# Attention with two accumulator banks for two query rows in turn, scores computed three chunks ahead, and the first loads in parts

## What is computed

```python
def mla_block_attend(qn, qp, kn, kp, v, qpos, kpos):
    s = jnp.einsum('bqhd,bkhd->bhqk', qn, kn) + jnp.einsum('bqhr,bkr->bhqk', qp, kp)
    s = jnp.where(chunk_mask(qpos, kpos), s.astype(F32) * MLA_SCALE, NEG_INF)
    p = jax.nn.softmax(s, axis=-1).astype(v.dtype)
    return jnp.einsum('bhqk,bkhd->bqhd', p, v)

def mla_prompt(q_nope, q_pe, ckv, kpe, w_ukv, pos):
    kv = jnp.einsum('bsl,lhe->bshe', ckv, w_ukv)
    k_nope, v = kv[..., :MLA_NOPE], kv[..., MLA_NOPE:]
    ...
    for i in range(q_nope.shape[1] // QBLK):
        lo, hi = i * QBLK, (i + 1) * QBLK
        outs.append(mla_block_attend(q_nope[:, lo:hi], q_pe[:, lo:hi], k_nope[:, :hi], kpe[:, :hi],
                                     v[:, :hi], pos[lo:hi], pos[:hi]))
```

## Time and profile before

| | us |
|---|---|
| median of 3 runs (lowest, highest) | 3652.87 (3643.95, 3655.99) |
| the profiled execution, its time | 3626.36 |
| its span | 3624.6 |
| attention stage: first load issued, first matmul, last output | 1550.3, 1566.0, 2300.8 |
| the steps of the first turn | 1585 to 1748.8 |
| TensorE busy, whole span | 3138.2 (87%) |
| VectorE busy, whole span | 1518.5 (42%) |

### The profile page before, as it was taken

One profiled execution on the slowest core, in us unless ns is written; L12 is line 12 of the kernel. 1 busy time (PEld: TensorE's weight loads), 2 busy tenths in 40 slices (PEclk: granted clock), 3 DMA queues, 4 the chain that ended last, 5 costly groups with the idle time before them and its releaser, 6 DMA issues. The chain is left out here.

```text
span 3624.6 us, 83086 instructions
## 1 busy us (share of the span) xinstructions
PE 3138.2 (87%) x31099; PEld 2434.5 (67%) x31100; DVE 1518.5 (42%) x3411; ACT 1060.9 (29%) x2630; POOL 499.9 (14%) x797
## 2 busy tenths in 40 slices
PE   5999999999999999669898989699809999999980
PEld 5988888888888888535555555355407776777660
DVE  0455555555455544458686868322320000000007
ACT  1333333333333333334434444122202222222220
POOL 0100111011011100100000000011142222222220
PEclk9999999999999999789999999899959999999995
DMA  5100000000000000020101010333218797773336
GB/s 168 28 25 25 25 25 25 28 25 25 25 25 25 27 25 25 22 61 1 35 1 35 1 33 1 120 127 129 102 49 282 230 349 236 250 231 80 82 64 214
DMA packets 136065, 297.66 MB, mean 82 GB/s; under 512 B 29404, under 2 KB 87038, under 8 KB 121342
## 3 DMA queue, kind: packets, MB, share of 16 engines
q1 hardware_dynamic: 113629, 215.78, 17.5%
q0 software_dynamic: 19520, 67.15, 8.0%
q10 hardware_dynamic: 2592, 9.96, 0.7%
HBM read 208.32 MB, written 84.53 MB: 81 GB/s over the span
## 5 line engine op out<-in xcount | busy, mean ns | idle before, releaser
L699 PE MATMUL mx_bank<-mx_xT,mx_w_in 128*128 128x128 f32 (+1 forms) x5440 | 677.3, 282 | 25.7 <-DMA mx_w_in<-in_w_in 25.2
L699 PEld LDWEIGHTS mx_bank<-mx_xT,mx_w_in 128*128 128x128 f32 (+1 forms) x5440 | 633.3, 191 | 92.9 <-issue 84.2
L1397 PE MATMUL at_bank<-at_kT,at_qT 128*128 128x512 f32 (+5 forms) x656 | 295.6, 537 | 2.4 <-DVE at_vals L1521 2.4
L1369 ACT ACTIVATE at_PQ<-at_bank,at_nms 128x512 f32<-128x512 f32 (+5 forms) x328 | 193.0, 596 | 280.4 <-DVE at_nms L1497 199.6
L2185 DVE SCALAR_TENSOR_TENSOR ex_th<-ex_th,ex_bank 128x256 f32<-128x256 f32 x64 | 26.9, 421 | 581.6 <-ACT ex_th L2101 581.6
L2172 PE MATMUL ex_bank<-ex_wd,ex_hT 128*128 x512 | 234.1, 600 | 2.1 <-ACT ex_hT L2107 2.1
L2152 PE MATMUL ex_bank<-ex_wg,ex_xT 128*128 x1024 | 234.6, 383 | 1.2 <-SPq L2022 1.2
L2152 PEld LDWEIGHTS ex_bank<-ex_wg,ex_xT 128*128 128x128 f32 x1024 | 196.6, 192 | 55.4 <-issue 31.3
L2152 PE MATMUL ex_bank<-ex_wu,ex_xT 128*128 x1024 | 231.5, 379 | 0.0
L1428 PEld LDWEIGHTS at_bank<-at_PT,at_vals 128*64 128x64 f32 (+1 forms) x2208 | 118.5, 138 | 160.5 <-issue 82.4
L1540 DVE COPY at_PT<-at_bank 128x512 f32<-128x512 f32 (+3 forms) x328 | 196.7, 601 | 57.1 <-PE at_bank L1409 43.1
(11 more groups left out here) (308 smaller groups left out, 5041.4 us busy)
## 6 DMA issues: line engine op xcount, KB each, us to landing
ex_wg<-in_w_eg SPq DMA_DIRECT2D x32, 1024.0 KB
ex_wu<-in_w_eu SPq DMA_DIRECT2D x32, 1024.0 KB
ex_wd<-in_w_ed SPq DMA_DIRECT2D x32, 1024.0 KB
mx_x<-in_x SPq DMA_DIRECT2D x19, 512.0 KB, 4.6
ro_x<-in_x SPq DMA_DIRECT2D x17, 512.0 KB, 3.7
scr_hx<-ro_h SPq DMA_DIRECT2D x17, 512.0 KB, 2.7
scr_acc<-ro_ha SPq DMA_DIRECT2D x17, 512.0 KB, 3.0
co_r<-scr_acc SPq DMA_DIRECT2D x17, 512.0 KB, 3.7
```

Of the source, the lines that this page charges most:

```text
L699: ins = pe.matmul(dst, w_in[:, k, col:col + n], xT[:, k, :], start=(k == 0), stop=(k == KC - 1))
L1369: ins = a.activation(PQ[:, n % NP, 0:full], b[:, 0:full], ACT.Exp, bias=bias, scale=SCALE, accum_out=sums[:, j, h, 1 + gi:2 + gi])
L1397: t.mark(pe.matmul(bank[n % SB][:, 0:wd], qT[h][keys(h), j * P:(j + 1) * P], kT[h][keys(h), k0 * P:k0 * P + wd], start=True, stop=True), f ...
```

## The change

Five things change, all in `attention`.

- Bank 6 becomes a second bank of sums: row j adds up in `bank[6 + j % 2]`, its reciprocals are turned in the same bank, and its first value product waits for `out_{j-2}`.
- The banks come from the scores: AHEAD = 3 and SB = 4, so step n issues S(n + 3) and max(n + 3).
- The transpose of the reciprocals moves from the step of the row's last pair to the step after it (`turned`), and with it ScalarE's copy and VectorE's output.
- The planner lets a row's pairs begin when the row before the last is out (`free.get(j - 2)`), not the last one. The plan that comes out has the same pairs in the same steps as before, but for row 16, whose two pairs move from step 86 to step 84.
- The 2 MB of latents come in four parts, each with a semaphore of its own, for which K0 to K3 wait one by one; K4 waits for the two small loads. SP issues the weights `w` first and then these loads; TensorE enters its loop without them, and waits for the rotary keys and the identity only before the first scores.

```diff
-    AHEAD, SB, TB = 4, 5, 2
+    AHEAD, SB, TB = 3, 4, 2
...
-        step = max(step, place[j, 1, g] + LAG, free)
+        step = max(step, place[j, 1, g] + LAG, free.get(j - 2, 0))
...
             row_end[step] = j
-            free = step + 2
-    steps = max(max(share) + 1, count)
+            turned[step + 1] = j
+            free[j] = step + 3
+    steps = max(max(share) + 2, count)
...
+        def summed(j):
+            return bank[6 + j % 2][:, 0:P]
+
+        def turned_sum(j):
+            return bank[6 + j % 2][:, P:2 * P]
...
+            def first_loads():
+                for k in range(4):
+                    cols = slice(512 * k, 512 * k + 512)
+                    sp.dma_start(lat[:, :, cols], lt[:, :, cols]).then_inc(lat_in[k], 16)
...
                                              io["w_ukv"][one][:, :, c * P:(c + 1) * P].rearrange("a p (k n) -> p (a k) n", k=2)))
+                if isinstance(t.i, int):
+                    first_loads()
...
         def _(pe):
-            pe.wait_ge(latents.sem, latents.done(0))
             pe.wait_ge(setup, 6)
...
-                            if j > 0:
-                                t.w(vec, f"out_{j - 1}")
+                            if j > 1:
+                                t.w(vec, f"out_{j - 2}")
                             else:
-                                t.w0(vec, last_out)
+                                t.w0(vec, f"out_{NT - 1 - (NT - 1 - j) % 2}")
...
+                    pe.wait_ge(lat_in[n], 16 if n < 4 else 32)
...
-                    if n in row_end:
-                        row_rec(t, row_end[n])
+                    if n in turned:
+                        row_rec(t, turned[n])
```

More of the change, by code:

```diff
@@ L1189, in attention @@
     pairs = [(j, g, s) for j in range(NT) for g in range(len(groups(j))) for s in range(groups(j)[g][1])]
-    share, row_end = {}, {}
-    step, free = 0, 0
+    share, row_end, turned = {}, {}, {}
+    step, free = 0, {}
     for i, (j, g, s) in enumerate(pairs):
-        step = max(step, place[j, 1, g] + LAG, free)
+        step = max(step, place[j, 1, g] + LAG, free.get(j - 2, 0))
         while share.get(step, 0) == BURST:
@@ L1197, in attention @@
         if i + 1 == len(pairs) or pairs[i + 1][0] != j:
+            while step in row_end:
+                step += 1
+            if step not in share:
+                share[step] = 0
             row_end[step] = j
-            free = step + 2
-    steps = max(max(share) + 1, count)
+            turned[step + 1] = j
+            free[j] = step + 3
+    steps = max(max(share) + 2, count)
     last_use = {n: max(m for m in range(count) if m % NP == n % NP) for n in range(NP)}
@@ L1218, in pv_names @@
                 out.append(f"PV{j}_{g}")
-        return out + ([f"recT{row_end[n]}"] if n in row_end else [])
+        return out + ([f"recT{turned[n]}"] if n in turned else [])
     def max_names(n):
@@ L1231, in out_names @@
     def out_names(n):
[L1232 removed]
+        return [f"out_{turned[n - 1]}"] if n - 1 in turned else []
     KV = [f"K{n}" for n in range(5)]
@@ L1269, in attention @@
             ("tensor", ten_names), ("vector", vec_names), ("scalar", act_names), ("gpsimd", pol_names)))
-        latents = Dmas(nc, ctx, "at_latents", 10)
+        latents = Dmas(nc, ctx, "at_latents", 7)
+        lat_in = [ctx.enter_context(nc.semaphore(f"at_lat_in{k}")) for k in range(5)]
         setup = ctx.enter_context(nc.semaphore("at_setup"))
@@ L1381, in turn @@
                             t.w0(vec, last_out)
-                        t.mark(a.activation(recb[:], bank[7][:, P:2 * P], ACT.Copy), f"rec{j}")
+                        t.mark(a.activation(recb[:], turned_sum(j), ACT.Copy), f"rec{j}")
             engine_loop(a, act, turns, turn)
@@ L1427, in values @@
                             for h, m in ((0, m0), (1, m1)):
-                                ins = pe.matmul(bank[7][64 * h:64 * h + 64, 0:P], vals[0:rows, k0 + s, 64 * h:64 * h + 64],
+                                ins = pe.matmul(summed(j)[64 * h:64 * h + 64], vals[0:rows, k0 + s, 64 * h:64 * h + 64],
                                                 PT[0:rows, m % NPT, s, :], start=(gi == 0 and s == 0), stop=end)
@@ L1436, in row_rec @@
                 t.w(vec, f"rec_wide{j}_1")
-                t.mark(pe.transpose(bank[7][:, P:2 * P], wide[:].rearrange("p a n -> p (a n)"), ident[:, :]), f"recT{j}")
+                t.mark(pe.transpose(turned_sum(j), wide[:].rearrange("p a n -> p (a n)"), ident[:, :]), f"recT{j}")
             def turn(t):
@@ L1459, in turn @@
                 t.w(vec, "V4")
+                pe.wait_ge(latents.sem, latents.done(0))
                 t.arrived(q_in)
@@ L1514, in output @@
                     t.left(o_out)
-                t.mark(v.tensor_tensor(o_sb[:, j, :], bank[7][:, 0:P], recb[:], ALU.mult), f"out_{j}")
+                t.mark(v.tensor_tensor(o_sb[:, j, :], summed(j), recb[:], ALU.mult), f"out_{j}")
             def turn(t):
```

25 lines of the change are left out of this document (12 added, 13 removed).

## The result

The changed kernel is slower: 3722.74 us in the median (3713.39 to 3727.43, 4 runs) against 3649.08 (3643.95 to 3655.99, 4 runs), a ratio of 1.020 (1.017 to 1.023). The forecast was 3687, with a range from 3650 to 3717. The direction was right; the loss of some 73 us is more than twice the 34 foreseen, and the time lies above the range.

The account below looks back on a forecast made before the run. TensorE and VectorE were taken to share the bound in attention. 45 + 13 - 16 - 2 - 5.6 = +34 us gave 3661 against the profiled execution, 3687 for a median run; range 3650 to 3717.

Parts of the forecast that it names:

- rows 8 to 11: Three-chunk half-rows, three ahead: TensorE waits for exp, 0.4 us at each of 32 places, +13 us, bounds 0 and 21.
- rival (d): Clock falls behind gaps of about 2.2 us at 16 head-1 starts: 26 more, +60, 3713 us; chance 0.19 with (c).
- The main term: Rows 12 to 15, scores three ahead: the chain starts one step later, +45 us over four turns, bounds 22 and 72.
- My decision mark: TensorE's gap at row 14's first chunk: under 1.2 us would show the main term wrong.
- The chain: Rows 12 to 15, a half-row's last scores through maximum, scaled maximum and exp to the transposes: about 3.0 us.
- Rival (a): The lead was never real: chains cost 22 us, rows 8 to 11 nothing, waits come back; -27, 3626 us; chance 0.11.
- (b): About the same: chains 1.2 us at 32 places, rows 8 to 11 at 0, larger gains; +5, 3658 us; chance 0.12.
- (c): Second bank's gains worth nothing because VectorE binds rows 0 to 7; +52, 3705 us; chance 0.19 with rival (d).
- The gain: TensorE's waits for the sums' bank and widened reciprocals, rows 0 to 7: -16 us; turns' ends: -2 us.
- The start: Loads in parts, weights first: first matmul at 1560.4 instead of 1566.04, 5.6 us saved once, bounds 1 and 7.

Follow-up runs that it names:

- e3: e1 plus products nobody reads, 384 columns wide, ahead of the first transposes of each half-row in rows 12 to 15; 3695.51 us, ratio 1.015.
- e19: The changed kernel plus products nobody reads, 384 columns wide, ahead of the first transposes of each half-row in rows 12 to 15; 3688.77 us, ratio 1.011.
- e10: The changed kernel with four chunks ahead, five score banks and one bank of transposes instead of two; 3673.41 us in one run.
- e11: The kernel before with one bank of transposes instead of two, still four chunks ahead; 3681.43 us in one run.
- e4: The kernel before with only the changed kernel's loads, latents in parts and weights first; 3639.17 us in a single run.
- e1: The kernel before with only three chunks ahead and four score banks (AHEAD, SB = 3, 4); 3712.65 us, ratio 1.021.

## Why the prediction was off

| us against before | forecast | measured without half clock |
|---|---|---|
| three chunks ahead (e3 beside before) | +45 +13 | +53: 44 in rows 12 to 15 and 16 in rows 8 to 11, less 4.5 ahead of a turn's first copy and 2 in rows 0 to 7 |
| second bank of sums, later reciprocals | -16 -2 | -8 (e19 beside e3), -6 (e10 beside e11) |
| loads in parts | -5.6 | -4 at the start, +3 to +4 at three turns' beginnings |
| sum | +34 | +44.6 (e19) |
| half clock | 0 (rival (d): +26) | +27.4 (the changed kernel beside e19) |
| | +34 | +72.0 |

What the slow scores of e3 and e11 themselves cost (3.7 and 3 us) is taken off. From its first scores to its last output a turn takes 174.7 us in e19, where 172 to 174 were foreseen, and 180.5 to 183.2 in the changed kernel.

**The main term was right.** The workings per half-row can be held against e19 and e3, where the clock stays up in these rows, from the transposes of one first chunk to those of the next as in the forecast: chunk 60 to 64 foreseen 8.5, measured 8.7 and 8.6; chunk 64 to 68 foreseen 9.8, measured 9.8 and 10.0. Rows 12, 13 and 15 of head 0 lose 1.46, 1.33 and 2.19 in e19 (foreseen 1.5, 1.3, 2.2). Rows 12 to 15 together: +43.7 against 45. My decision mark, a gap over 1.2 us at row 14's first chunk, came out at 2.05; the gaps of head 1 are 2.0 to 2.2, as foreseen. The chain was 0.66 us longer than the 3.0 I had worked out, since VectorE had a copy more in front of the last maximum. Rival (a), that the lead was never real, falls with it. So does (b).

**That rows 8 to 11 fit is luck.** I took 13 us for them, and e19 shows 13.2. But the kernel before has two slow scores a turn in these rows and takes 45.07 us there; e4, the same kernel in these rows, has none and takes 43.5. Beside e4 the lost lead costs 22 us (e1), just over my upper bound of 21, and e19 loses 19; four falls that went away hid 6 of it. I had 0.4 us for each half-row; the gaps in e19 are 1.0 to 1.5 us at head 0 and up to 0.4 at head 1.

**The step that failed is the clock, which stands at nothing in the sum.** It measured +27.4 us. My only reason for leaving it out stands in rival (d), on the gap of 2.33 us ahead of row 7: "after the same wait in the other turns it did not fall". That was misread. The trace of before has, in the second turn,

```profile
1821.71 0.88 PE L1428 MATMUL at_bank<-at_PT,at_vals 128*64 128x128 f32 x12 [2.32 <-DVE at_o_sb L1515]
1822.52 1.11 PE L1409 MATMUL at_bank<-at_ident,at_PQ 128*128 128x128 f32 x4
1823.43 1.91 PE L1397 MATMUL at_bank<-at_kT,at_qT 96*128 96x512 f32 x2
```

What misled me is the first row: the value products right behind the gap still run at full clock (0.88, where the first turn has 1.19), the transposes 0.8 us later take 1.11 instead of 0.65, and the slow scores come 1.7 us later. The gap of 2.73 ahead of row 0's reciprocals does the same:

```profile
1596.12 0.33 PE L1437 MATMUL at_bank<-at_ident,at_wide 128*128 128x128 f32 x1 [2.73 <-DVE at_wide L1509]
...
1597.37 1.92 PE L1397 MATMUL at_bank<-at_kT,at_qT 128*128 128x512 f32 x2
```

Slow scores stood behind both gaps in all four turns of before, eight places of eight. That was evidence for (d), which I priced at 26 and gave a chance of 0.19 together with (c). With (d) in the forecast it would have been 3713, 10 us from what was measured. That its size came out so near is partly luck too: I had 16 falls of 1.6 us, one behind each of the 16 first chunks of head 1. There were 18, some 1.5 us each, and 12 of them lie behind first chunks of head 0, where the gaps are 1.4 to 2.85 us, and only 6 behind those of head 1.

**The gain was put too high.** I took 16 us for waits in rows 0 to 7 and 2 for the turns' ends. Measured are 6.2 less in rows 0 to 7, but of these 2 belong to three ahead (e1) and 2 to the later reciprocals. The Trainium skill ("Perfetto Trace Analysis", Optimization Strategy) says that a repeated gap on the engine that should be saturated can mean too little PSUM; by that rule alone the term would have been 42. The trace agrees that the bank was what TensorE waited for, but not that its time comes back: the wait for the sums' bank fell by 22 us and the one for the widened reciprocals by 8, and 6 to 8 us of time came of it. The engines share the bound there, and VectorE had less to give than I counted. Of the 5.3 us a turn that I read as its waits, only the 1.8 of the earlier trace rows lie in rows 0 to 7; the rest comes behind 1637.68, where its copies for row 8 begin. In the changed kernel the same wait is, in rows 0 to 7 of the first turn,

```profile
DVE at_PT L1561 <- PE at_bank L1428: 0.2, 1, 0.2
```

so VectorE has nothing left to give there, and these rows are 1.5 us a turn shorter. TensorE's gaps did not vanish there, they changed their cause: 3.5 us are now waits for exp and 2.4 for copies.

**The start** saved 5.0 us to the first matmul (foreseen 5.6) and 3.9 to the first scores, since the five key groups now take longer:

```profile
1578.06 1.92 SPq L1325 DMA_DIRECT2D at_w<-in_w_ukv  x4
...
1584.24 11.01 PE L1466 MATMUL at_bank<-at_lat,at_w 128*128 128x512 f32 x20 [21.68 <-DMA at_lat<-scr_ckvT]
```

The first quarter of the latents took 4.2 us from issue to the first matmul (foreseen 3.6), and the five groups 11.01 us instead of the 9.93 of the earlier trace rows. That the later turns begin 3 to 4 us later in sum was not foreseen, and is not explained.

## What to carry to other kernels

Where a step needs the result of several chunks (a maximum over a half-row), the lookahead in chunks is worth more than a bank for sums: count what lies between the last scores and the first transposes, and price it before giving a bank away. Once a gap of some 2 us on TensorE is in the forecast, look at the products two to four rows behind every gap of that size that the trace already has, in every turn, and put the clock into the sum where they are slow. A large wait of one engine is no gain by itself while the engine it waits for is nearly full: see first how long that one stands in the same rows.

## What the runs showed of the hardware

The clock does not follow the length of the gap alone. In the changed kernel chunk 68 of row 14 has a gap of 2.06 us in each of the four turns, and only in the third are scores slow behind it; and within a few microseconds of one turn:

```profile
1712.92 0.82 PE L1428 MATMUL at_bank<-at_ident,at_PQ 128*128 128x128 f32 x4 [1.98 <-ACT at_PQ L1389]
1713.54 1.91 PE L1416 MATMUL at_bank<-at_kT,at_qT 96*128 96x512 f32 x2
...
1731.82 0.65 PE L1428 MATMUL at_bank<-at_ident,at_PQ 128*128 128x128 f32 x4 [2.10 <-ACT at_PQ L1389]
1732.31 1.02 PE L1416 MATMUL at_bank<-at_kT,at_qT 96*128 96x512 f32 x2
```

A gap of 1.98 us is followed by half clock, one of 2.10 is not. e1 is plainer still, in its first turn:

```profile
1694.85 0.65 PE L1409 MATMUL at_bank<-at_ident,at_PQ 128*128 128x128 f32 x4 [2.99 <-ACT at_PQ L1369]
1695.34 1.02 PE L1397 MATMUL at_bank<-at_kT,at_qT 128*128 128x512 f32 x2
...
1730.66 0.75 PE L1409 MATMUL at_bank<-at_ident,at_PQ 128*128 128x128 f32 x4 [1.86 <-ACT at_PQ L1369]
1731.20 1.92 PE L1397 MATMUL at_bank<-at_kT,at_qT 128*128 128x512 f32 x2
```

In each of its first three turns the longest gap, 2.99 us, and those of 2.09 to 2.30 leave the clock up, and the gaps of 1.86 and 1.82 bring it down. In rows 12 to 15 of e3 and e19, where the longest gap is 1.5 us, there is no slow score. Which gaps bring the fall is therefore left open; that it varies with small shifts of the whole (e4 beside before) makes some 6 us of noise in this stage. The Trainium skill ("TensorE: Matmul & The Clock Gate", A second HAM failure mode: psum-queue depth-cycling) tells of a bf16 kernel that turned through PSUM banks and whose short idles between groups of matmuls made the clock go to and fro. The trace agrees in the effect: in rows 12 to 15 the granted clock is 0.89 to 0.93 with gaps of 1.4 to 2.85 us. Here the gaps are waits for exp, not a turning through banks.
